# A two-layer mixer and mixture-of-experts trunk: who normalises the input stream, and the order around the layer boundary

## The reference, cut to what matters

```python
def layer_norm(x, g, b):
    mu = mean(x); var = mean((x - mu)**2)
    return (x - mu) * rsqrt(var + LN_EPS) * g + b

h = layer_norm(x, ln_in_g, ln_in_b)                       # "ln0"
for l in range(DEPTH):                                    # DEPTH = 2
    m = hybrid_mixer(h, ..., w_in[l], ...)                # first: z = h @ w_in
    h = layer_norm(ALPHA * h + m, ln1_g[l], ln1_b[l])     # "ln1"
    f = grouped_moe(h, ..., w_gate[l], w_up[l], w_down[l])  # top 2 of 32 experts
    h = layer_norm(ALPHA * h + f, ln2_g[l], ln2_b[l])     # "ln2"
return h
```

## Time and profile before

| | us |
|---|---|
| median of 3 runs (lowest, highest) | 2278.38 (2276.97, 2281.16) |
| the profiled execution | 2278.19 |
| its span in the profile | 2276.4 |
| TensorE busy, matmul | 2056.1 (90%) |
| VectorE busy | 956.1 (42%) |
| ScalarE busy | 674.4 (30%) |
| GpSimd busy | 195.4 (9%) |

### The profile page before, as it was taken

One profiled execution on the slowest core, in us unless ns is written; L12 is line 12 of the kernel. 1 busy time (PEld: TensorE's weight loads), 2 busy tenths in 40 slices (PEclk: granted clock), 3 DMA queues, 4 the chain that ended last, 5 costly groups with the idle time before them and its releaser, 6 DMA issues.

```text
span 2276.4 us, 29903 instructions
## 1 busy us (share of the span) xinstructions
PE 2056.1 (90%) x10000; PEld 1226.0 (54%) x10000; DVE 956.1 (42%) x1930; ACT 674.4 (30%) x1390; POOL 195.4 (9%) x244
## 2 busy tenths in 40 slices
PE   6999999999979988788989999999998799887887
PEld 4777876877743333222357678668777333222232
DVE  6865845645651111011178667555456411110113
ACT  4345544544210000000043536546551010000000
POOL 3000001000011111111000000010001111111110
PEclk9999999999989999989999999999999899999999
DMA  6221321323489999999833112113235999999996
GB/s 206 75 75 38 111 75 38 111 75 121 167 336 421 425 424 426 426 426 424 330 132 111 38 61 102 61 38 111 75 130 198 406 424 425 425 425 425 426 422 244
DMA packets 96420, 535.58 MB, mean 235 GB/s; under 512 B 13936, under 2 KB 16880, under 8 KB 73472
## 3 DMA queue, kind: packets, MB, share of 16 engines
q1 hardware_dynamic: 84288, 510.41, 55.6%
q0 software_dynamic: 11968, 23.11, 2.7%
HBM read 527.17 MB, written 23.07 MB: 242 GB/s over the span
## 4 chain that ended last, share of the span: by engine, by line
PE 73%; DVE 9%; issue 6%; DMA 6%; ACT 3%; another core or an unknown queue 2%; POOL 0%; DVEq 0%; SPq 0%; POOLq 0%; ACTq 0%
PE ps L1060 18%; PE ps L757 11%; PE ps L759 11%; PE ps L758 11%; PE ps L1078 9%; DMA scr<-in_w_up 4%; PE ps L856 2%; PE ps L907 2%; PE ps L878 2%; PE ps L1050 1%; DVE scr L2081 1%; DMA scr<-h_rows,scr 1%; ACT scr L1273 1%; PE ps L1162 1%
## 5 line engine op out<-in xcount | busy, mean ns | idle before, releaser
L2061 DVE COPY scr<-ps 128x512 f32<-128x512 f32 x64 | 44.3, 692 | 746.9 <-PE ps L1050 746.9
L757 PE MATMUL ps<-hT_lo,w_hi 128*128 128x512 f32 (+1 forms) x816 | 328.6, 403 | 7.2 <-DVE w_lo L1541 4.8
L759 PE MATMUL ps<-hT_hi,w_hi 128*128 128x512 f32 (+1 forms) x816 | 318.9, 391 | 0.0
L758 PE MATMUL ps<-hT_hi,w_lo 128*128 128x512 f32 (+1 forms) x816 | 317.8, 389 | 0.0
L1061 PE MATMUL ps<-scr 128*64 128x512 f32 x480 | 233.7, 644 | 0.0
L1230 ACT ACTIVATE scr<-ps 128x512 f32<-128x512 f32 (+1 forms) x200 | 103.7, 519 | 327.7 <-PE ps L1078 308.9
L1250 ACT ACTIVATE w_hi<-ring 128x1024 fp32r<-128x1024 f32 x122 | 129.2, 1059 | 224.8 <-PE ps L759 190.8
L1541 DVE TENSOR_TENSOR w_lo<-ring,w_hi 128x1024 fp32r<-128x1024 f32 x122 | 149.2, 1223 | 104.4 <-ACT w_hi L1250 99.8
L1482 ACT ACTIVATE scr<-ps 64x512 f32<-64x512 f32 x64 | 37.7, 589 | 522.2 <-PE ps L1061 522.2
L757 PEld LDWEIGHTS ps<-hT_lo,w_hi 128*128 128x128 f32 (+1 forms) x816 | 153.0, 187 | 42.0 <-DVE w_lo L1541 5.0
L759 PEld LDWEIGHTS ps<-hT_hi,w_hi 128*128 128x128 f32 (+1 forms) x816 | 152.8, 187 | 34.0
(11 more groups left out here) (262 smaller groups left out, 3420.2 us busy)
## 6 DMA issues: line engine op xcount, KB each, us to landing
ring<-in_w_down SPq DMA_DIRECT2D x32, 2048.0 KB, 45.7
ring<-in_w_in SPq DMA_DIRECT2D x30, 2048.0 KB, 8.0
scr<-in_w_up SPq DMA_DIRECT2D x28, 2048.0 KB, 46.3
xslot<-in_w_down SPq DMA_DIRECT2D x26, 2048.0 KB, 50.4
spare<-in_w_gate SPq DMA_DIRECT2D x16, 2048.0 KB
ring<-in_w_gate SPq DMA_DIRECT2D x16, 2048.0 KB, 43.6
ring<-in_w_up SPq DMA_DIRECT2D x16, 2048.0 KB, 47.7
wslot<-in_w_up SPq DMA_DIRECT2D x14, 2048.0 KB, 50.8
```

The lines of the kernel that those rows point to most:

```text
L757: mm(out, a[0], b[1], start=first, stop=False)
L758: mm(out, a[1], b[0], start=False, stop=False)
L759: return mm(out, a[0], b[0], start=False, stop=last)
```

## The change

**Norms ln0 and ln2.** VectorE keeps the first step (less the mean, times `g`). ScalarE multiplies by the root, in a new `scale`, one instruction of 128x1024 a tile. The offset `b` is then missing in `h`. For the turned rows TensorE adds it: behind each transpose a product of one row (128 values of `b`, against ones) goes onto the same 128x128 of the bank. For the stream itself VectorE adds `b` later: four additions of 128x1024 at the start of each layer, ahead of all else there, and four after the last layer, each ahead of its tile's DMA out.

**Start of a layer.** `index_logits` makes the product of tiles 0 to 2 (384 columns) behind a new semaphore of `take_hT`, then that of tile 3 (128 columns). TensorE waits for the two first weight units one by one, and no longer for banks 0 to 3.

**Boundary.** TensorE turns tile 0 ahead of the returned rows of tile 3. VectorE splits the two first weight units ahead of the statistics, and normalises a tile right behind its own statistics. The products of L752 are four, of 256 columns, behind tile 2. SP loads `h` before the norm's parameters, and `index_weights` of the next layer right behind these, not behind `got`.

**Experts.** Gate and up of expert 30 come in quarters too, and `idle_products(5)` is gone. An expert beyond its capacity uses slots 1 to 3, not 0 to 2.

```diff
@@ SP, tail
+                    def gate_up_quarters(e, landed):
+                        gate_s, up_s = (slots[expert_slot(e, m)] for m in range(2))
+                        for m in range(2):
+                            used(piece_ahead(piece_no[e, m]))
+                        for q in range(4):
+                            cut = slice(q * UNIT, (q + 1) * UNIT)
+                            for w, s in ((w_gate, gate_s), (w_up, up_s)):
+                                sp.dma_start(s[:, cut], w[one, e:e + 1].rearrange("o q p c -> p (o q c)")[:, cut]
+                                             ).then_inc(landed[q].sem, landed[q].tick("gu", 16))
                     for n in range(XRING, 3 * EPT - 3):
+                        if PIECES[n] == (EPT - 2, 0):
+                            gate_up_quarters(EPT - 2, near_gu)
+                        if PIECES[n][0] == EPT - 2 and PIECES[n][1] < 2:
+                            continue
...
+                    gate_up_quarters(EPT - 1, last_gu)
...
+                    used(H_LAST)
+                    sp.dma_start(h[:, :, :], h_rows.rearrange("(t p a) c -> p t (a c)", p=P, a=2)).then_inc(
+                        h_back.sem, h_back.tick("h", 16))
                     used(LN_LAST)
...
-                    used(H_LAST)
-                    sp.dma_start(h[:, :, :], h_rows.rearrange("(t p a) c -> p t (a c)", p=P, a=2)).then_inc(
-                        h_back.sem, h_back.tick("h", 16))
+                    used(max(n for n in range(3 * EPT) if SLOT_OF[n] == in_slot["idx"]))
+                    with sp.If(l < DEPTH - 1):
+                        index_weights(slice(DEPTH - 1, DEPTH), "idx next")
                     multiplied(("y", EPT - 1))
...
-                    with sp.If(l < DEPTH - 1):
-                        index_weights(slice(DEPTH - 1, DEPTH), "idx next")
...
-                    sp.wait_ge(h_ready.sem, h_ready.at(("ln2", t), DEPTH - 1))
+                    sp.wait_ge(out_ready.sem, out_ready.at(("out", t)))
@@ TensorE
+                            if key != "ln1":
+                                ins = mm(bank[b].t[:, k * P:(k + 1) * P], ln_params[key][1][0:1, kd * P:(kd + 1) * P],
+                                         ident[0:1, 0:1].to_broadcast([1, P]), start=False, stop=True,
+                                         skip_group_check=True)
...
-                        for w in range((0, 0, 2, 4)[t]):
+                        for w in range((0, 0, 4, 0)[t]):
...
-                            mm(bank[6 if key == "ln0" else c_bank(0, 0)].t, ident, h[:, t, 0:512], start=True,
+                            mm(bank[6 if key == "ln0" else c_bank(0, 0)].t[:, 0:2 * P], ident, cf[:, 0:2 * P], start=True,
...
+                    for cut in (slice(0, (NT - 1) * P), tok(NT - 1)):
+                        if cut.start:
+                            pe.wait_ge(hT_ready.sem, hT_ready.start(l))
+                        for k in range(KD):
+                            ins = split_product(bank[b].t[0:KEY_W, cut], w(k), hT(k, cut), k == 0, k == KD - 1)
...
-                        if e == EPT - 3:
-                            idle_products(5, i)
...
-                    for t in range(NT):
+                    for t in range(NT - 1):
                         returned(t, l)
-
                     with pe.If(l < DEPTH - 1):
-                        transpose_h("ln2", l)
+                        transpose_tile("ln2", 0, l)
+                    returned(NT - 1, l)
+                    with pe.If(l < DEPTH - 1):
+                        transpose_h("ln2", l, 1)
@@ ScalarE
+                def scale(key, t, l=0):
...
+                    nc.scalar.activation(h[:, t, :], h[:, t, :], ACT.Copy, scale=rstd[:, t:t + 1]).then_inc(
+                        h_ready.sem, h_ready.tick((key, t)))
...
-                take_hT("ln0", tiles=range(0, 2))
-                split_first("pre")
-                take_hT("ln0", tiles=range(2, NT))
+                for t in range(NT + 1):
+                    if t < NT:
+                        scale("ln0", t)
+                    if t >= 1:
+                        take_hT("ln0", 0, (t - 1,))
+                    if t == 2:
+                        split_first("pre")
@@ VectorE, start of a layer
+                    dve.wait_ge(h_ready.sem, h_ready.start(l))
+                    for t in range(NT):
+                        V.tensor_tensor(h[:, t, :], h[:, t, :], ln_params["ln0"][1], ALU.add).then_inc(
+                            h_full.sem, h_full.tick("h"))
```

More of the change, by code:

```diff
@@ L373, in trunk @@
         last_gu = [signal(f"last_gu{q}") for q in range(4)]
+        near_gu = [signal(f"near_gu{q}") for q in range(4)]
         last_down = [signal(f"last_down{q}") for q in range(4)]
@@ L670, in _ @@
                     last = slice(EPT - 1, EPT)
[L671 to L678, removed]
+                    down_s = slots[expert_slot(EPT - 1, 2)]
+                    gate_up_quarters(EPT - 1, last_gu)
                     used(piece_ahead(3 * EPT - 1))
@@ L1051, in turn_rows, with gate_up @@
                     return ins
-                def gate_up(n, slots, b, last_of=None):
+                def gate_up(n, slots, b, last_of=None, landed=last_gu):
                     wg, wu = cols(slots[0]), cols(slots[1])
@@ L1102, in gates @@
                         if e < EPT - 1:
-                            slots = [piece_landed(e, m) for m in range(2)]
-                            free(2 + 2 * n, l, i)
-                            filled(gate_up(n, slots, 2 + 2 * n), 2 + 2 * n, ("gu", e))
+                            if e < EPT - 2:
+                                slots = [piece_landed(e, m) for m in range(2)]
+                                free(2 + 2 * n, l, i)
+                                ins = gate_up(n, slots, 2 + 2 * n)
+                            else:
+                                slots = [expert_slot(e, m) for m in range(2)]
+                                free(2 + 2 * n, l, i)
+                                ins = gate_up(n, slots, 2 + 2 * n, l, near_gu)
+                            filled(ins, 2 + 2 * n, ("gu", e))
                             expert_rows(e + 1, xin_land[(e + 1) % 2].start(l, i) + 16 * ((e + 1) // 2), l, i)
@@ L1149, in over_block @@
                     pe.wait_ge(over_hT.sem, over_hT.value("over", 1, 0, b))
-                    down(0, 2, 6).then_inc(over_y.sem, over_y.tick())
+                    down(0, 3, 6).then_inc(over_y.sem, over_y.tick())
                     pe.wait_ge(over_ye.sem, over_ye.value("over", 1, 0, b))
@@ L1188, in _ @@
                     book.scope = "layer"
-                    for b in range(4):
-                        pe.wait_ge(bank[b].read, bank[b].full.now(l))
                     index_logits(l)
@@ L1252, in split_to @@
                         split[0] += 1
+                def scale(key, t, l=0):
+                    if key == "ln2":
+                        for half in range(2):
+                            in_sbuf(c_bank(t, half), ("c", t, half), l)
+                    else:
+                        act.wait_ge(centred.sem, centred.at((key, t), l))
+                    act.wait_ge(rstd_ready.sem, rstd_ready.at((key, t), l))
+                    nc.scalar.activation(h[:, t, :], h[:, t, :], ACT.Copy, scale=rstd[:, t:t + 1]).then_inc(
+                        h_ready.sem, h_ready.tick((key, t)))
                 def split_first(when, l=0):
@@ L1512, in _ @@
                     with act.If(l < DEPTH - 1):
-                        take_hT("ln2", l, range(0, 2))
                         split_first("next", l)
-                        take_hT("ln2", l, range(2, NT))
+                    for t in range(NT + 1):
+                        if t < NT:
+                            scale("ln2", t, l)
+                        if t >= 1:
+                            with act.If(l < DEPTH - 1):
+                                take_hT("ln2", l, (t - 1,))
             @block.vector
@@ L1553, in take_hT, with alone_inc, split_first @@
                                         hT_hi[:, dst[0], dst[1]].bitcast(F32), ALU.subtract).then_inc(bank[b].read, 1)
-                def split_first(when, l=0):
-                    for q in range(2):
+                    dve.wait_ge(bank[b].read, bank[b].full.at((key, t, 1), l))
+                    dve.wait_ge(bank[b - 1].read, bank[b - 1].full.at((key, t, 0), l))
+                    alone_inc(hT_ready, (key, t))
+                def alone_inc(sig, key):
+                    dve.sem_inc(sig.sem, sig.tick(key))
+                def split_first(when, l=0, parts=range(2)):
+                    for q in parts:
                         dve.wait_ge(hi_ready.sem, hi_ready.at((when, q), l))
@@ L1589, in normalise @@
                                                    ALU.subtract, ALU.mult).then_inc(bank[b].read, 1)
-                        for half in range(2):
-                            in_sbuf(c_bank(t, half), ("c", t, half), l)
-                    else:
```

(21 more changed lines are left out.)

29 lines of the change are left out of this document (15 added, 14 removed).

## The result

The changed kernel takes **2318.82 us** (median of 4 runs, 2317.93 to 2320.1), the kernel before on the same chip 2277.68 (2276.91 to 2281.16): ratio 1.0176, 95% interval 1.0163 to 1.019. That is slower, where I had forecast 2268. The profiled execution took 2317.93, with a span of 2316.2.

The account below looks back on a forecast made before the run. TensorE, holding 73% of the chain of waits, was taken to bound the kernel, with DMA landings or VectorE in places. Terms -4.1 - 4.2 + 0.9 + 0.3 - 2.9 - 1.6 + 1.0 = -10.6 gave 2268 us; range 2263.5 to 2279.

Parts of the forecast that it names:

- a pair is 0.33, a tile 2.7 us: Boundary, TensorE: a transpose plus one-row product takes 0.33 us, a turned tile of eight such pairs 2.7 us.
- Rival 2: Turned tiles: transpose and one-row product do not overlap, 0.82 us a pair, total 2295, slower above 0.50; chance 0.12.
- Rivals 1 and 2: The first: TensorE at half clock (1.2 GHz) in input norm and boundary, +8.8 us, total 2276.4, chance 0.20.
- Input norm: Start of the kernel, to the end of the index keys: 40.8 us instead of 39.81, +1.0.
- Last experts, layer 0: Gate and up of expert 31 end at 1107.3 instead of 1111.4, set by the last quarter's landing: -4.1 us.
- Last experts, layer 1: Gate and up of expert 31 end at 2229.0 instead of 2233.2, reckoned as in layer 0: -4.2 us.
- To the first returned row: Layer 0 after the last experts: `got` queues behind index weights, +0.9; VectorE may meet weights late, +0.3 us.
- Boundary: First returned row to first index-query product: 33.0 us instead of 35.9, -2.9, VectorE keeping up.
- The additions on VectorE: Layer start: four additions, 4.9 us, fall in VectorE's idle time and cost nothing; uncovered, 4.9 a layer.
- End: After TensorE's last record: VectorE finishes 7.8 us later instead of 9.5; -1.6 us (0 to -2).

Follow-up runs that it names:

- e4: Changed kernel with the input norm's one-row products writing the unread bank, so offsets are left out there: 2319.15 us.
- e3: Changed kernel with 128-row offset products instead of one-row ones: 2273.94 us (10 runs), ratio to before 0.9968.
- e10: Repeat, on one chip with e9, of the changed kernel with 128-row offset products and no unread products in the boundary: 2272.40 us, ratio 0.9966.
- e9: Repeat of the changed kernel with 128-row offset products, on one chip with e10: 2274.23 us, ratio to before 0.9966.
- e8: Changed kernel with 128-row offset products and no unread products in the boundary: 2271.77 us, ratio to before 0.9955.
- e7: Kernel before, with only gate and up of expert 30 in quarters and the five unread products removed: 2276.87 us, ratio 0.9979.
- e2: Changed kernel with four transposes, then four one-row products in each bank, instead of alternating: 2389.71 us, with changed data.
- e1: Changed kernel without the one-row offset products: 2314.24 us, with changed data and one more overflow block of experts.
- e5: Changed kernel with 64-row offset products instead of one-row ones: 2311.62 us (one run).
- e6: Changed kernel with 32-row offset products instead of one-row ones: 2320.24 us (one run).

## Why the prediction was wrong

**The step that failed** is "a pair is 0.33, a tile 2.7 us" in the boundary's part. I took the spacing of neighbours that all use 128 rows for a product with one row between two such neighbours, and wrote that the nearest row decides. It was the nearest in columns, not in what mattered. The pair measured 0.67 us at full pace and 1.13 at half.

**Rival 2** went in the right direction, with chance 0.12. Its price of 0.82 us a pair was near (0.67), and the threshold it named, 0.50, was crossed. Its cause was wrong: e4 excludes a wait for the transpose's result, e3 shows that a product that adds onto it can flow. Its argument against (attention's mixed transposes and products flow) did not ask whether those change the number of rows. The Trainium skill's rule on tiling modes, above, speaks against this change, and I had not weighed it; by it the rival was the likelier case.

**Rivals 1 and 2 came together**, which I had not considered: I gave them as alternatives. The one-row pairs stayed at half pace or fell to it, and half pace makes them cost more. From my own sum: 64 pairs at 0.34 more make 21.8 us, to 2289. The rest, by rows: 40 of the pairs at half pace and three in part, together 19.1 us more, of which my forecast already held 2.6 for the first tile, so 16.5; the unread products twice some 1.8 more; the index keys partly at half pace, 1.6 and 1.7 us; and the mixers, +1.5 and +3.0 in the table, which have nearly the same waits as before. That is some 28 us, to about 2317, against the measured 2318.8. It is a reckoning, not a test: no run had one-row pairs at full pace throughout, and the terms below were off too.

**Input norm** (+1.0): +22.5 in the change. With 128 rows it was +0.5, with the first index-query product at 40.32 against my 40.8. The pace rose there 3.5 us after the first transpose, within the first tile; I had put it at that tile's end. In the other traces with 128 rows it rose 4.4 (e10), 5.4 (e9) and 5.8 us (e8) after it, with the first index-query product of e9 at 41.88.

**Last experts, layer 0** (-4.1, end at 1107.3): right. In the changed kernel the delay shrinks from 24.3 us at the first gate and up to 20.5, so 3.8. Reckoned in the same way it is 2.9 in e3 (3.9 earlier at the end, 1.0 at the start), 5.0 in e7, 4.6 in e8, 4.0 in e9 and 4.5 in e10.

**Last experts, layer 1** (-4.2): too large. 1.7 in the change (43.3 to 41.6), 1.9 in e3 and e8, 2.5 in e7, 2.8 in e9, 2.3 in e10. In the change, e7 and e10 TensorE waits for the last quarter's landing there, as I said, but that landing came later than my term had it. In e3, e8 and e9 it waits for no quarter in that layer; it had waited before, 1.7 to 2.0 us, for the `down` piece of an expert before it (`ring<-in_w_down`, 2048 KB). Why the landings came later is open. The pace of the quarters was as assumed: 409 to 415 GB/s over the last 20 us or so before them, in either layer of the change, e3 and e7. So the Trainium skill's figure of 341 GB/s for 1 MB alone (DMA: Bandwidth & Descriptors, Bandwidth) was again not what pieces of 512 KB that follow each other ran at, as in the earlier trace rows.

**To the first returned row** (+1.2 together): -0.6. From the end of the last gate and up to the first returned row it took 18.5 us before, 17.9 in the change and 17.9 in e3.

**Boundary** (-2.9): +19.9 in the change. In e3 it was 35.5 us instead of 35.9 and not 33.0. Of the 2.5 us missing, 2.0 are the idle time ahead of layer 1's index keys. I had the work of TensorE there and its waits for other engines, but not that the loop turns. By these rows eight unread products behind the last turned tile covered it in the kernel before (5.6 us from that tile's first transpose to the keys), and the slow pairs in the changed one (6.7 us).

**The additions on VectorE** (0): right. TensorE's waits for other engines in layer 0's mixer are the same to 0.1 us; 0.6 us came to them without a releaser (L889). Of the changed kernel (waited for, total, times, longest), and of the kernel before:

```profile
PE ps L777 <- DVE w_lo L1589: 2.4, 2, 1.9
```

```profile
PE ps L757 <- DVE w_lo L1541: 2.4, 2, 1.9
```

**End** (-1.6, VectorE 7.8 us behind TensorE): 7.2 us in both the change (2305.42 to 2312.66) and e3, from 9.5; the way out took 3.5 instead of 3.0, so -1.7.

```profile
2306.73 1.40 DVE L1643 SCALAR_TENSOR_TENSOR h<-ps,moments,scr 128x512 f32<-128x512 f32 x2
2308.04 4.62 DVE L2179 TENSOR_TENSOR h<-h,scr 128x1024 f32<-128x1024 f32 x4
```

So e3 has the pair that I had priced, at 0.335 us. That its profiled execution took 2268.82 us, against my 2267.6, is in part luck: the two tails gave 1.2 and 2.3 us less than forecast and the boundary 2.5 less, while the two mixers, of which I had nothing, gave 2.5 and the way to the first returned row 1.7 more. And it was the fastest of its ten runs; the median, 2273.94, stands 6.7 us below before's on that chip, where the forecast had 10.6.

## What to carry to other kernels

A product of fewer than 128 rows between instructions of 128 rows is not cheap, however small it is: two changes a pair cost 0.34 us at full and 0.49 at half pace, the clock fell while such pairs ran, and 64 of them undid a change whose other edits gain 6.7 us at the medians. Give such a product all rows (here the operand lay on all partitions already), or group it with its like where the sum allows it (in e2 the result changed). When an instruction has no row in the trace, compare it with its neighbours in every dimension, partitions too; and where two rivals share a place, price them together.

## What the runs showed that I had not expected

- 64, 32 and 1 rows cost the same 0.67 and 1.13 us a pair; 128 rows 0.335 and 0.64.
- TensorE's pace stayed at half (1.2 GHz) for 27 us of unbroken one-row pairs (17.1 to 44.1), and also with one-row products in groups (16.7 to 35). With 128-row products it rose 3.5 to 5.8 us after the first transpose (e3 at 21.2, e8 at 24.1), and with transposes alone (e1) not until after 28, behind unread products from 24.55 on. The eight unread products behind the third tile ended in a rise in the changed kernel and in e5, and in none in e4 and e6. What brings the rise these runs do not settle.
- The turn of the loop over layers, as I read it, leaves TensorE without work for 1.9 to 3.9 us (e10, e3, e9, e8, e1) unless work of its own queued ahead covers it. The keys of layer 1 began 4.8 to 5.0 us behind tile 3's first transpose in all five.
- Without the offsets in both norms' turned rows (2% of the stream's size) the residual of layer 1 began 47 us later and 6.5 MB more were read, an overflow block more. Without those of the input norm alone (e4) the bytes read stayed the same.
